# Chunks 8 to 15 of the first experts loaded before the block boundary, and the later rounds' slot products placed behind the six turns

## The reference

```python
def hier_moe(h, w_rg, b_rg, w_re, b_re, w_gate, w_up, w_down):
    ...
    g_logit = (hf @ w_rg).astype(jnp.float32) + b_rg
    g_sel = jnp.argmax(g_logit, axis=-1)
    ...
    top_v, top_i = lax.top_k(e_logit, TOP_K)
    gate = jax.nn.softmax(top_v, axis=-1) * g_p[:, None]
    ...
    def expert_block(args):
        xb, e = args
        return (jax.nn.silu(xb @ w_gate[e]) * (xb @ w_up[e])) @ w_down[e]

    yb = lax.map(expert_block, (xin, blk_e)).reshape(P, D)
    out = jnp.zeros((T + 1, D), jnp.float32).at[row_t].add(yb.astype(jnp.float32) * row_w[:, None])[:T]
```

## Time and profile before

| | us |
|---|---|
| median of 3 runs | 3497.9 |
| the runs | 3494.2 to 3506.98 |
| the profiled execution | 3497.66 |
| its span in the profile | 3495.9 |
| PE busy in the span | 3372.7 |
| stage `experts`, from the barrier at about 2953.6 to the end | 542 |

### The profile page before, as it was taken

How to read it: one execution, slowest core, us unless ns; L and a number is a source line. 1 busy time by engine, 2 the same in 40 slices (tenths; PEclk the granted TensorE clock), 3 DMA queues, 4 the chain that set the end, 5 groups by cost and what they waited for, 6 DMA issues and landing times. The chain is left out here.

```text
span 3495.9 us, 47733 instructions
## 1 busy us (share of the span) xinstructions
PE 3372.7 (96%) x19782; PEld 2518.1 (72%) x19782; DVE 1754.1 (50%) x2882; ACT 993.1 (28%) x1312; POOL 329.2 (9%) x333
## 2 busy tenths in 40 slices
PE   8999999999999999999999999999999998999999
PEld 6888888756878888887858888877787875333333
DVE  4746557538665368566797433455434433121122
ACT  2112111437422233222325322343435432000001
POOL 2000000200120002000231200000000002312210
PEclk9999999999999999999999999999999998999999
DMA  7423223210244334455352222231321334999996
GB/s 281 143 75 121 97 94 107 69 60 1 73 145 138 113 122 145 145 181 167 97 149 73 97 93 100 79 114 49 97 85 61 115 127 169 381 419 414 410 417 266
DMA packets 322186, 532.08 MB, mean 152 GB/s; under 512 B 20626, under 2 KB 277347, under 8 KB 296112
## 3 DMA queue, kind: packets, MB, share of 16 engines
q1 hardware_dynamic: 308720, 512.19, 41.2%
q0 software_dynamic: 9840, 12.93, 1.1%
q10 hardware_dynamic: 3408, 3.89, 0.4%
HBM read 516.01 MB, written 21.05 MB: 154 GB/s over the span
## 5 line engine op out<-in xcount | busy, mean ns | idle before, releaser
L521 PE MATMUL banks<-operand_hi,trunk_weights_hi 128*128 128x512 f32 (+1 forms) x1568 | 565.9, 361 | 22.9 <-DVE trunk_weights_lo L1353 11.5
L521 PE MATMUL banks<-operand_lo,trunk_weights_hi 128*128 128x512 f32 (+1 forms) x1568 | 557.9, 356 | 0.0
L521 PE MATMUL banks<-operand_hi,trunk_weights_lo 128*128 128x512 f32 (+1 forms) x1568 | 557.8, 356 | 0.0
L521 PEld LDWEIGHTS banks<-operand_hi,trunk_weights_hi 128*128 128x128 f32 x1568 | 297.9, 190 | 72.9 <-DVE trunk_weights_lo L1353 13.1
L4558 PE MATMUL banks<-expert_room,x_rows 128*32 128x512 f32 x1920 | 334.6, 595 | 0.5 <-DVE x_rows L4434 0.5
L521 PEld LDWEIGHTS banks<-operand_lo,trunk_weights_hi 128*128 128x128 f32 x1568 | 298.1, 190 | 41.8
L521 PEld LDWEIGHTS banks<-operand_hi,trunk_weights_lo 128*128 128x128 f32 x1568 | 297.5, 190 | 41.9
L1353 DVE TENSOR_TENSOR trunk_weights_lo<-weight_ring,trunk_weights_hi 128x2048 fp32r<-128x2048 f32 x90 | 206.0, 2289 | 163.5 <-ACT trunk_weights_hi L1308 163.5
L521 PE MATMUL banks<-trunk_hidden_hi,trunk_weights_hi 128*128 128x512 f32 (+1 forms) x672 | 233.1, 347 | 4.1 <-DVE X L1379 1.7
L1308 ACT ACTIVATE trunk_weights_hi<-weight_ring 128x2048 fp32r<-128x2048 f32 x90 | 171.7, 1907 | 215.6 <-PE banks L521 215.5
L521 PE MATMUL banks<-trunk_hidden_hi,trunk_weights_lo 128*128 128x512 f32 (+1 forms) x672 | 230.9, 344 | 0.0
(11 more groups left out here) (627 smaller groups left out, 6228.8 us busy)
## 6 DMA issues: line engine op xcount, KB each, us to landing
weight_ring<-ffn_w SPq DMA_DIRECT2D x120, 1024.0 KB, 4.9
weight_ring<-w_mod SPq DMA_DIRECT2D x72, 1024.0 KB, 4.9
expert_room<-w_gate SPq DMA_DIRECT2D x40, 1024.0 KB, 17.5
expert_room<-w_up SPq DMA_DIRECT2D x40, 1024.0 KB, 16.9
expert_room<-w_down SPq DMA_DIRECT2D x40, 1024.0 KB, 18.3
weight_ring<-w_in SPq DMA_DIRECT2D x26, 1024.0 KB, 5.0
weight_ring<-w_gate SPq DMA_DIRECT2D x16, 1024.0 KB, 17.1
weight_ring<-w_down SPq DMA_DIRECT2D x16, 1024.0 KB, 19.0
```

Of the source, the lines that this page charges most:

```text
L521: ins = pe.matmul(bank[:, at:at + width], w, x[:, at:at + width], start=start and n == 0, stop=stop and n == len(passes) - 1)
```

## The change

Four things are changed; the arithmetic is the same.

1. `at_slot` and `later_rows` move to operand piece 7, and `first_ids` gets a buffer of its own. So only chunk 13's home is held by slot operands.
2. SP issues chunks 8 to 12, 14 and 15 in `project_and_route`, ahead of the barrier. In `experts` it no longer waits for the gathers; it waits for `s_later` and issues chunk 13 alone.
3. PE runs all six turns and then LATER. DVE copies all six halves and then makes the later slot numbers.
4. Since LATER's bank is also that of set 1's up product, PE waits for `s_ids` ahead of phase 2 of set 1, in every unit.

```diff
@@ -3859,13 +3859,13 @@
         XR = sb("x_rows", [P, ST, D])
         gates, chances = sb("gates", [P, 2, ST]), (sb("chosen_ratio", [P, ST]), sb("group_sums", [P, ST]))
         pairs = sb("pairs", [P, 1], I32)
+        first_ids = sb("first_ids", [P, 2 * ST, QUADS * SETS], F32R)
         HR = sb("rt_h_rows", [P, ST, D])
         ids, tokens = sb("slot_ids", [P, ROUNDS * QUADS * SETS], U32), sb("slot_tokens", [P, ROUNDS * QUADS * SETS], U32)
         with ExitStack() as early:
             operands = early.enter_context(nc.sbuf_tensor("so_operands", [P, 8, SLOT], F32R))
-            slot_rows = (operands[:, 4, 0:2 * ST * P].rearrange("p (j l) -> p j l", l=P),
-                         *(operands[:, 5, 2 * ST * QUADS * at:2 * ST * QUADS * to].rearrange("p (j c) -> p j c", j=2 * ST)
-                           for at, to in ((0, SETS), (SETS, NB))))
+            slot_rows = (operands[:, 7, 0:2 * ST * P].rearrange("p (j l) -> p j l", l=P), first_ids,
+                         operands[:, 7, 2 * ST * P:2 * ST * (P + QUADS * (NB - SETS))].rearrange("p (j c) -> p j c", j=2 * ST))
         with ExitStack() as late:
             last_rows = late.enter_context(nc.sbuf_tensor("last_rows", [P, 10, SLOT], F32R))
         room = sb("expert_room", [P, 10, SLOT])
@@ -3966,7 +3966,10 @@
             for t in range(ST):
                 sp.wait_ge(s_ca, 2 * t + 2)
                 sp.dma_start(k.rows_dram[t * P:(t + 1) * P, :], HR[:, t, :]).then_inc(s_rows, 16)
-            for c in range(8, 10):
+            for c in range(8, 13):
+                load_expert_chunk(k, sp, 0, c, 0)
+            sp.wait_ge(s_t, 2 * ST)
+            for c in (14, 15):
                 load_expert_chunk(k, sp, 0, c, 0)
             sp.wait_ge(s_rows, 16 * ST)
 
@@ -4275,11 +4278,8 @@
                             load_expert_chunk(k, sp, 0, QUAD * (f - 2) + j, 8 * ((p + 1) % 4))
             first = last_round(sp)
             n = first + LAST
-            for s in range(SETS):
-                sp.wait_ge(s_xg[s], 16)
             sp.wait_ge(s_later, 1)
-            for c in range(10, ROOM):
-                load_expert_chunk(k, sp, 0, c, 0)
+            load_expert_chunk(k, sp, 0, 13, 0)
             sp.wait_ge(s_gates, 1)
             sp.dma_start(k.gates_dram.rearrange("(c t p) o -> p c (t o)", c=2, p=P), gates[:], allow_slow_non_contiguous=True).then_inc(s_gd, 16)
             with sp.Fori(0, first + 1) as p:
@@ -4491,11 +4491,9 @@
                 link(dve.reciprocal(gates[:, 0, :], gates[:, 0, :]))
                 link(dve.tensor_tensor(gates[:, 0, :], gates[:, 0, :], sums[:], ALU.mult))
                 dve.tensor_tensor(gates[:, 1, :], gates[:, 0, :], ratio[:], ALU.mult).then_inc(s_gates, 1)
-            x_out(0)
-            x_out(1)
+            for i in range(6):
+                x_out(i)
             later_ids()
-            for i in range(2, 6):
-                x_out(i)
             chosen_gates()
             dve.wait_ge(s_lane_of, 4)
             dve.wait_ge(s_spread, 256)
@@ -4585,6 +4583,8 @@
                 for s in range(SETS):
                     phase(1, s, p, u)
                 for s in range(SETS):
+                    if s == 1:
+                        pe.wait_ge(s_ids, 1)
                     pe.wait_ge(s_yb, of(p, u, SETS, s + 1))
                     phase(2, s, p, u)
                 phase(3, 0, p, u)
@@ -4631,11 +4631,10 @@
             for i in range(6):
                 if i >= 2:
                     pe.wait_ge(s_xc, 2 * i - 2)
-                if i == 2:
-                    for j in range(2 * ST):
-                        ins = pe.matmul(LATER, at_slot[:, j, :], later_rows[:, j, :], start=j == 0, stop=j == 2 * ST - 1)
-                    ins.then_inc(s_later, 1)
                 turn_x(i)
+            for j in range(2 * ST):
+                ins = pe.matmul(LATER, at_slot[:, j, :], later_rows[:, j, :], start=j == 0, stop=j == 2 * ST - 1)
+            ins.then_inc(s_later, 1)
             first = last_round(pe)
             n = first + LAST
             with pe.Fori(0, first + 1) as p:
```

## The result

The changed kernel takes 3502.32 us (median of 17 runs, 3498.89 to 3509.57), the kernel before 3497.81 in 17 runs beside them. The ratio is 1.0016, with a 95% interval of 1.0009 to 1.0022, that is +3.1 to +7.7 us. The two medians themselves are 4.5 us apart. It is slower, but within 0.5%: what the prediction called no change that counts, and inside its range.

The account below looks back on a forecast made before the run. It took PE to bound the experts, with only the start before them able to move. 3497.66 + 5.0 (turn 2 later) + 1.96 (LATER) - 1.0 (clock) + 0.2 (s_ids waits) = 3503.8 us; range 3498 to 3510.

Parts of the forecast that it names:

- a stage ahead that differs by over 2 us: Sign of being wrong in kind: a stage ahead of the experts differing by over 2 us.
- Case B: Rival at the barrier: gathers hardly feel the loads, leaving LATER; +1 to +4 us, 3499 to 3502; chance 0.28.
- Case E: Rival, faster: start as before and the clock loss vanishes; -1, 3496.5; chance 0.05.
- The wait of the barrier: Before the turns: gather 0, slowed by loads in flight, lands and opens the barrier 3.0 us later; bounds 0 and 8.9.
- The equal share: DMA engines go round queues by packets; by equal share alone gather 0, beside SP's loads, would lose nothing.
- Gather 1: Set 1's gather, behind the barrier, slowed until the loads end: 2.0 us more before turn 2.
- Case C: Rival at the barrier: gathers wait out the loads, turn 2 8.4 late; sum +9.6, 3507.2; chance 0.11.
- LATER, 1.96: Between last turn and first expert product: LATER, no longer hidden by the wait for gather 1, adds 1.96 us; bound 1.4.
- The clock: PE's half-clock loss of 2.1 us after the first product shrinks by 1.0; ends -2.1 and 0.
- The waits on s_ids: PE's eight added dynamic waits, ahead of phase 2 of set 1: 0.2 us taken, at most 0.4.
- The later slot numbers: DVE's later numbers come 12 us later, most of it coming back with loads gone: cost 0, up to 12 without cover.
- Chunks 10 to 15 early: In the experts: weight chunks there early remove nothing, since nobody waits for them.

Follow-up runs that it names:

- e4: The changed kernel with POOL issuing the gather of set 0 behind the barrier, first of the three; ratio 1.0014 against the kernel before.
- e5: The kernel before with POOL issuing the gather of set 0 behind the barrier, first of the three; ratio 1.0002 against the kernel before.
- e2: The kernel before with only LATER and the later slot numbers moved behind all turns and the s_ids waits added; ratio 1.0003 against the kernel before.
- e3: The changed kernel with chunks 8 to 11 ahead of the barrier and 12 to 15 behind the gathers; ratio 1.0006 against the kernel before.
- e8: The changed kernel with one later-slot instruction repeated 12 times more on DVE, about 4 us; ratio 1.0012 against the kernel before.
- e1: The changed kernel with LATER and the later slot numbers back between sets 0 and 1, without the s_ids waits; ratio 1.0011 against the kernel before.
- e7: The kernel before with idle products alone added on PE (small matmuls whose result nobody reads); ratio 0.9994 against the kernel before.
- e9: The kernel before with all three gathers ahead of the barrier, LATER behind all turns and idle products on PE; ratio 0.9988 against the kernel before.
- e12: The same kernel as e9, run again; ratio 0.9989 against the kernel before.

## Why the prediction was right, and where it wasn't

The forecast was +6.1 on the profiled execution, 3503.8 us; the runs give +5.6 (3.1 to 7.7) by the ratio and 4.5 by the medians, the median 3502.32. The stage alone gives +3.7, which the interval allows too. Whether the 1.9 us between stage and ratio are anything, the runs don't settle. The changed kernel's profiled execution took 3504.12 us, next to the 3503.8 forecast, and that is luck: 2.8 of its 6.5 us stood ahead of this stage, and what the sum forecast there, 6.2, was 3.7. The prediction had named a stage ahead that differs by over 2 us as a sign of being wrong in kind. The sign came, by up to 4.3 us, and is read above as a difference between executions. Case B, +1 to +4, fits the stage's 3.7 as a number; it is the drain of 9.59 that rules it out, since B has 5.3. Case E's -1 does not follow from its own words (the start as before and 2.1 us of clock back are -2.1), and nothing hangs on it.

Within the sum:

- **The wait of the barrier, 3.0, was 4.3** (9.59 against 5.31). The mechanism was right: the drain waits for gather 0 (e4, e5), and the gather shares with the loads. The size came from the 84 quarter gathers; gather 0 carries all the rows at once, and its 0.41 MB at a quarter of the engines' time take 4 us instead of 2.8, behind 3 us in which it moved nothing. The equal share that would have led to case B is there by packets, 80 and 80, and is a quarter by bytes.
- **Gather 1, 2.0, was 0.9** (3.88 against 3.03). The loads had some 2.5 us left when it was issued, forecast 4.0, since the barrier came later than forecast. The two misses cancel: turn 2 came 5.2 us later, forecast 5.0. Case C, where the gather waits out the loads, would have had a drain over 13.
- **LATER, 1.96, was 0.5.** From the last turn to the first product it is 1.02 us instead of 0.55. The 0.55 do pass beside LATER, which I had named as a bound (1.4) and not taken, and part of it already ran at 2.4 GHz. In e2, at half clock, it was 1.0, below that bound too, since LATER itself took 1.59 us in this place and not 1.96.
- **The clock, -1.0, was -2.06** (37.90 against 39.96): the end of the range that I had given. Which end it is does not follow from the change. The loss was whole in e2 and e3 (39.89 and 40.01) and gone in e4, e5 and e8 (37.90, 37.97, 37.90), with PE's work ahead of the first product nearly the same. In e1 the clock was back too, with 0.9 us lost otherwise.
- **The waits on s_ids, 0.2, were 0.** A quad takes the same 64.0 us, and the way from the 352 records to the end is equal to 0.1 us.
- **The later slot numbers: cost 0 was right, the reason wrong.** I said that most of the 12 us would come back with the loads out of the way. Nothing came back: behind the first round's slot numbers the later ones were done 10.5 us later (22.0 against 11.5), from there to DVE's scaling it took 33.3 us instead of 27.9, and quad 1's last copies began at 3028.37 instead of 3012.84, 12.8 us later behind the slot numbers and 7.1 behind the first product. The loads were out of the way: from 2976 to 2984 SP's queue moved 0.00 MB. But ACT issued its 16 loads only at 2984.39, when its store had landed, 12.3 us behind the store's issue. DVE waited 10.2 us for the quarter gathers where it had waited 1.3. What held was the slack: quad 1's first product was at 3034.81, and its third set is turned last and needed last.
- **Chunks 10 to 15 early won nothing**, as said: PE waited for no chunk before and for none now.

## What to carry to other kernels

A wait that keeps bulk loads off the queues while a small gather is under way can be worth more than the early loads, if nothing waits for these: look in the chain first for who does. POOL's drain at this barrier waited for its gather in flight (9.59 us), while SP's, with its loads in flight until 2964, took 7 ns: look in the trace whose drain waits, for what that engine issues just ahead of a barrier sets when everyone goes on. And where PE stands in such a stage, its clock is part of the price. A cheap filler in the wait gave 2.5 us by the stage alone (e7, not clear of noise in the runs) and, together with all gathers ahead of the barrier, 4 us that the runs show (e9, e12).

## What the runs showed of the hardware that was not expected

**A gather beside queued loads waits before it shares.** Gather 0 moved its first byte 3 us behind the end of its issue, then took 23 to 29% of the DMA engines' time beside SP's queue. The Trainium skill, "DMA: Bandwidth & Descriptors", section "Queues, rings and completion order", has the engines go round their queues by packets. The trace agrees: from 2956 to 2958 there are 80 packets of either queue, and loads landed behind the gather. As the gather's packets are smaller, equal turns were a quarter of the time. The 3 us at the start (1.9 in e3, with two loads) are not in that rule, and what they are was not tried; in quiet the gather's packets began 0.4 us behind the issue.

**Set 1's gather is small in bytes and not in packets.** It took 3.0 us in quiet, 3.9 and 5.5 as the loads ran out, and 10.5 in e4, where set 0's was still under way in the same queue. Set 0's gather is 144 packets (before, 2950 to 2954), and those of sets 1 and 2 are 288 together (2956 to 2958) with some 0.02 MB. In quiet the 288 pass in 2 us. In e4, from 2965 to 2968, POOL's queue got 176 packets through beside 161 of SP's, under 60 a us, and set 1's gather landed 3.2 us behind set 0's. That fits a queue in which each gather's packets follow those of the one ahead and take turns with the loads'; no run separates the two.

**PE's issue can thin out for some microseconds in every quad.** On the chips of e9 to e12 the kernel before took 3558.75 and 3549.04 us instead of 3498 to 3500. A window of 64 us in e9, then the same window of the kernel before in its profile above:

```profile
3100.00:3164.00 64.00, 60.63 (x516) 21.04 (x512) 9.88 (x17) 4.79 (x8) 14.97 (x17) 1.00 0.89 359
```

```profile
3100.00:3164.00 64.00, 64.00 (x592) 19.67 (x588) 10.57 (x18) 5.37 (x9) 15.47 (x17) 1.00 1.02 417
```

516 product records instead of 592 at the same clock, and the DMA engines less busy, not more. The chain there has groups of four records every 1.4 us and puts the gaps down to issue:

```profile
3044.68 1.34 PE banks L4555 x5
3046.15 1.05 PE banks L4555 x4
3047.57 1.05 PE banks L4555 x4
```

What starves it was not looked into. It falls on the kernel before as on the others, so the ratios stand.
